# First queries and keys of three branches made as block products, their placing behind the last merge, and a first projection tile that begins with the high parts

## What is computed

```python
def token_mixer(x, w_in, b_forget, sinks, w_branch, w_gate, b_gate, w_out):
    (aq, ak, av, bq, bk, bv, cq, ck, cv, ciq, cik, ciw, dq, dk, dv, df) = jnp.split(x @ w_in, offsets, axis=-1)
    o_a = banded_attention(...)      # sliding window, 8 query heads, 2 key heads
    o_b = dilated_attention(...)     # three dilations, 8 heads
    o_c = dsa_attention(...)         # top 256 keys by an indexer, one key head for 8 queries
    o_d = forgetting_attention(...)  # causal, with a cumulative log forget gate
    proj = jnp.einsum('bsnk,nkd->bsnd', branches, w_branch)
    gates = jax.nn.sigmoid(x @ w_gate + b_gate).reshape(b, L, N_BRANCH, D_MODEL)
    merged = jnp.sum(gates * proj, axis=2)
    return merged @ w_out

def reference(x, ...):
    x = layer_norm(DEEPNORM_ALPHA * x + token_mixer(x, ...), ln1_g, ln1_b)
    return layer_norm(DEEPNORM_ALPHA * x + conv_glu_ffn(x, ...), ln2_g, ln2_b)
```

## Time and profile before

| | |
|---|---|
| median of 3 runs | 2093.48 us (2091.12 to 2094.64) |
| profiled execution | 2093.97 us, its span 2092.2 us |
| mean granted clock of PE | 0.999 |
| PE busy | 2060.4 us, 98% |
| DVE, ACT, POOL busy | 1536.4, 968.5, 937.3 us |
| share of PE in the chain that ended last | 87% |

### The profile page before, as it was taken

The page is one execution under the profiler, slowest core; times in us unless marked ns, Lnnn a source line. Parts: engine busy times, 40 slices in busy tenths (PEclk is TensorE's granted clock), DMA queues, the critical chain, the costliest instruction groups (busy, mean ns, idle before and its releaser), DMA issues.

```text
span 2092.2 us, 28999 instructions
## 1 busy us (share of the span) xinstructions
PE 2060.4 (98%) x10382; PEld 1727.0 (83%) x10382; DVE 1536.4 (73%) x2549; ACT 968.5 (46%) x1740; POOL 937.3 (45%) x796
## 2 busy tenths in 40 slices
PE   9999999999999999999999999999999999999998
PEld 7788888888888888888888888888788888888887
DVE  8678887777686666797785666668877777775668
ACT  5543334566615556615635666523433333344540
POOL 4287752333322223324523333524756565645651
PEclk9999999999999999999999999999999999999999
DMA  4233323110042111230031000441566665558862
GB/s 132 72 111 110 101 91 62 31 31 21 26 152 64 50 32 51 75 100 28 22 121 31 21 21 11 141 161 61 180 181 203 191 192 161 171 189 310 270 215 92
DMA packets 197373, 224.26 MB, mean 107 GB/s; under 512 B 25704, under 2 KB 149608, under 8 KB 197232
## 3 DMA queue, kind: packets, MB, share of 16 engines
q1 hardware_dynamic: 194320, 212.43, 32.7%
q10 hardware_dynamic: 2912, 10.00, 1.3%
HBM read 164.17 MB, written 58.23 MB: 106 GB/s over the span
## 4 chain that ended last, share of the span: by engine, by line
PE 87%; DVE 7%; issue 2%; ACT 2%; POOL 1%; DMA 0%; DVEq 0%; ACTq 0%; POOLq 0%
PE pair L1359 13%; PE pair L927 13%; PE pair L911 7%; PE pair L1225 7%; PE obank L1359 5%; PE pair L1388 5%; PE obank L1021 4%; PE chunk L1000 4%; PE pair L1318 3%; PE chunk L1388 3%; PE obank L1225 3%; PE pair L972 3%; PE pair L973 3%; PE pair L1271 2%; PE obank L1388 2%
## 5 line engine op out<-in xcount | busy, mean ns | idle before, releaser
L2175 POOL TENSOR_TENSOR w_lo<-w_raw,w_hi 128x1024 fp32r<-128x1024 f32 x64 | 159.5, 2492 | 311.1 <-ACT w_hi L1652 311.0
L1675 ACT ACTIVATE pt_hi<-chunk 128x512 fp32r<-128x512 f32 (+1 forms) x272 | 150.8, 555 | 179.2 <-PE chunk L1000 177.8
L2578 DVE TENSOR_TENSOR pt_lo<-chunk,pt_hi 128x512 fp32r<-128x512 f32 (+1 forms) x272 | 173.2, 638 | 80.1 <-ACT pt_hi L1675 75.7
L2230 POOL TENSOR_SCALAR prob<-prob,att 128x256 f32<-128x256 f32 (+4 forms) x172 | 118.1, 696 | 198.5 <-DVE att L2514 198.2
L927 PE MATMUL pair<-act_hi,w_hi 128*128 128x512 f32 x432 | 186.4, 432 | 2.5 <-DVE heads L2519 2.3
L927 PE MATMUL pair<-act_hi,w_lo 128*128 128x512 f32 x432 | 170.0, 393 | 0.0
L927 PE MATMUL pair<-act_lo,w_hi 128*128 128x512 f32 x432 | 169.4, 392 | 0.0
L2399 DVE TENSOR_SCALAR_CACHE_REDUCE o_top<-score,stat 128x384 uint8<-128x384 f32 (+1 forms) x186 | 167.0, 941 | 0.5
L1021 PE MATMUL obank<-pt_hi,heads 128*128 128x256 f32 (+1 forms) x568 | 148.4, 285 | 0.6 <-DVE pt_lo L2578 0.6
L1777 ACT ACTIVATE prob<-prob,att 128x257 f32<-128x257 f32 (+6 forms) x172 | 120.5, 702 | 39.3 <-DVE att L2504 38.0
L1021 PE MATMUL obank<-pt_lo,heads 128*128 128x256 f32 (+1 forms) x568 | 138.6, 281 | 0.0
(11 more groups left out here) (489 smaller groups left out, 5932.5 us busy)
## 6 DMA issues: line engine op xcount, KB each, us to landing
down_sums<-dn_sums SPq DMA_DIRECT2D x40, 512.0 KB, 6.4
w_raw<-in_w_in SPq DMA_DIRECT2D x37, 512.0 KB, 3.8
gates<-o_t SPq DMA_DIRECT2D x22, 512.0 KB, 2.9
up_raw<-in_w_up SPq DMA_DIRECT2D x22, 512.0 KB, 4.8
gate_raw<-in_w_ffn_gate SPq DMA_DIRECT2D x22, 512.0 KB, 6.0
hidden<-gelu_s SPq DMA_DIRECT2D x22, 512.0 KB, 3.3
dn_raw<-down_sums SPq DMA_DIRECT2D x44, 256.0 KB, 4.1
h_in<-down_sums SPq DMA_DIRECT2D x44, 256.0 KB, 4.8
```

The costliest lines, as they stand in the source:

```text
L2175: nc.gpsimd.tensor_tensor(split_into(1, g), w_raw[:, g % 2, 0:kt * cols], split_into(0, g).bitcast(F32), ALU.subtract).then_inc(lo_ready, 1)
L2578: nc.vector.tensor_tensor(pt_lo[:, n % PT_SLOTS, 0:m], t[:, 0:m], pt_hi[:, n % PT_SLOTS, 0:m].bitcast(F32), ALU.subtract).then_inc(chunk_f ...
```

## The change

Six more tiles join `GATE_TILES`: for D, A and C the first pair's queries and the first pair's keys (for C the keys and values), so that `NGATE` is 14. ACT copies them without the sigmoid, SP stores them in a tensor `first_heads` and loads the two of a branch back into `o_t[:, 0]` and `o_t[:, 1]` during the merge before. The steps `q`, `k` and `kv_c` of D, A and C become one step `heads`, in which PE does nothing: behind the last matmul of a merge it goes straight to the value tile (D, A) or to the transposes (C). ACT and DVE place high and low parts from `o_t` in pieces, and PE waits for the semaphore `first_placed` ahead of the scores of units 0, 4 and 8.

Around this, the last gated tile of B's, D's and A's merge is done by DVE behind the first placed pieces; gate tiles 6 and 7 go to other places of `o_t` and are loaded later; ACT's `ahead()` in the value step of D and A stands between the exponentials of units 0 and 1, and in C ahead of them; A's first bias lies elsewhere; the whole top-k search is done in the gates stage and the distances in the merges. C's filler table loses four parts, and nine instead of four go ahead of its first units. In `project_parts` the mode `low_last` sorts each half by product: all high by high, then high by low, then low by high, each with a wait of its own.

The core of the diff:

```diff
-TOPK_GATES = {1: 2, 6: 2, 2: 2, 5: 2, 7: 2, 3: 2, 4: 2}
-TOPK_MERGE = {B: (2, 3), D: (1, 2), A: (0, 1), C: (0, 0)}
-TOPK_FIRST = {("k", D): 7, ("q", D): 6, ("k", A): 5, ("q", A): 5}
-SEARCH_PARTS = 191
-DISTANCE_PARTS = 6
+TOPK_GATES = {1: 3, 6: 2, 2: 2, 5: 2, 7: 2, 3: 2, 4: 2}
+SEARCH_PARTS = 191 + NSC
+DISTANCE_PARTS = 5
+MERGE_ROWS = {B: 3, D: 2, A: 1}
+MERGE_PARTS = {B: (8, 2), D: (4, 1), A: (3, 1)}
...
-BESIDE_C = (((0, 0), (0, 2), (1, 1), (1, 1), (2, 2), (3, 0), (3, 1), (6, 0), (6, 2), (8, 1),
+BESIDE_C = (((0, 0), (3, 0), (3, 1), (6, 0), (6, 2), (8, 1),
...
-FIRST_C = 4
+FIRST_C = (4, 5)
...
-GATE_TILES = [(br, dt) for br in BRANCH_ORDER for dt in STORED_GATES[br] if (br, dt) not in FILLER_GATES]
+HEAD_TILES = [(what, br) for br in BRANCH_ORDER[1:] for what in ("q", "k")]
...
-        if br == C:
-            out += [("kv_c",)]
-        if br == A:
-            out += [("k", A, 0)]
-        out += [("q", br, 0)]
-        if br in (B, D):
-            out += [("k", br, 0)]
+        out += [("q", br, 0), ("k", br, 0)] if br == B else [("heads", br)]
         out += [("v_c",)] if br == C else [("v", br, 0)]
...
-                        order.sort(key=lambda kn: kn[1] == 2)
+                        order.sort(key=lambda kn: kn[1])
...
-                        if low_last and s == 0 and (k, n) == (0, 2):
+                        if low_last and (k, n) == (0, 0):
+                            pe.wait_ge(act_part, NTOK if s == 0 else 2 * NTOK)
+                        elif low_last and (k, n) == (0, 1):
+                            pe.wait_ge(*((x_taken, NTOK) if s == 0 else (x_low, NTOK)))
...
-                    fill(FIRST_C)
+                    fill(FIRST_C[0])
+                    pe.wait_ge(first_placed, placed_first(br, 1))
                     scores(br, pr, 0)
                     scores(br, pr, 1)
+                    fill(FIRST_C[1])
...
+                        if p == 0 and br != B and u in (4, 8):
+                            pe.wait_ge(first_placed, placed_first(br, u // 4 + 1))
...
+            def load_heads(br):
+
+                at = BRANCH_ORDER.index(br) - 1
+                if at == 0:
+                    sp.wait_ge(merge_free, 4)
+                else:
+                    sp.wait_ge(sum_done, sums_of(BRANCH_ORDER[at]) + 4)
+                for what in ("q", "k"):
+                    tile = GATE_TILES.index((what, br))
+                    sp.wait_ge(gate_stored[tile % 2], 16 * (tile // 2 + 1))
+                    sp.dma_start(first_head(what), tile_kept((what, br))).then_inc(heads_loaded, 16)
 
             def load_gate_tile(br, dt):
...
+            def gate_made_of(n, k, dst, src):
+
+                tile = GATE_TILES[2 * n + k]
+                if tile in HEAD_TILES:
+                    return nc.scalar.activation(dst, src, ACT.Copy)
+                return nc.scalar.activation(dst, src, ACT.Sigmoid, bias=gate_bias_of(*tile))
...
+            def first_heads(br):
+
+                at = BRANCH_ORDER.index(br)
+                act.wait_ge(merge_full, NKT * at)
+                act.wait_ge(heads_loaded, 32 * at)
+                first_half(br, 0)
+
+            def first_half(br, s):
+
+                q_hi(br, 0, 0, first_head("q")[0:HD, half_cols(s)], half_cols(s))
+                k_hi(0, first_head("k")[0:HD, half_cols(s)], cols=half_cols(s))
+
+            def other_heads(br):
+
+                first_half(br, 1)
+                q_hi(br, 0, 1, first_head("q")[HD:P, :])
+                if br != C:
+                    k_hi(1, first_head("k")[HD:P, :])
+                if br == D:
+                    act.wait_ge(merge_free, merge_at(B) + NKT)
+                    spill(NKT - 1)
+                if br == C:
+                    ahead()
+
...
                     tiles[1].next()
-                    for u in range(2):
-                        exps(step[1], step[2], u)
+                    exps(step[1], step[2], 0)
+                    if step[1] != B:
+                        ahead()
+                    exps(step[1], step[2], 1)
...
+                    gated(A, NKT - 1)
                     inverse(br, 0)
+                    first_half(br, 1)
                 if pr == 0:
                     biased(br, pr, 2)
                     biased(br, pr, 3)
+                if (br, pr) == (C, 0):
+                    other_query(br).then_inc(first_placed, 1)
                 if beside_v(br, pr):
...
+            def first_half(br, s):
+
+                q_lo(br, 0, 0, first_head("q")[0:HD, half_cols(s)], half_cols(s))
+                k_lo(0, first_head("k")[0:HD, half_cols(s)], cols=half_cols(s)).then_inc(first_placed, 1)
+
...
+                elif kind == "heads":
+                    first_half(step[1], 0)
+                    if step[1] != C:
+                        first_half(step[1], 1)
+                        gated(BRANCH_ORDER[BRANCH_ORDER.index(step[1]) - 1], NKT - 1)
...
+                    biased(step[1], step[2], 0)
+                    if step[1] != B:
+                        other_query(step[1])
+                        k_lo(1, first_head("k")[HD:P, :], (0,))
+                    biased(step[1], step[2], 1)
+                    if step[1] != B:
+                        k_lo(1, first_head("k")[HD:P, :], (1,)).then_inc(first_placed, 1)
+                    inverse(step[1], 0)
```

More of the change, by code:

```diff
@@ L794, in gate_bias_of, with tile_weights, tile_kept, first_head @@
             return gate_bias[:, br * NKT + dt:br * NKT + dt + 1]
+        def tile_weights(tile):
+            if tile not in HEAD_TILES:
+                return w_tile(w_gate[0], tile[0] * D_MODEL + tile[1] * P, P)
+            what, br = tile
+            return w_tile(w_in[0], Q_COL[br] if what == "q" else CK if br == C else K_COL[br], P)
+        def tile_kept(tile):
+            return heads_dram[HEAD_TILES.index(tile)] if tile in HEAD_TILES else gates_dram[tile]
+        def first_head(what):
+            return o_t[:, 0 if what == "q" else 1, :]
+        def placed_first(br, part):
+            return 3 * (BRANCH_ORDER.index(br) - 1) + part
         gate_out = [o_t[:, 2, :], o_t[:, 3, :]]
@@ L1073, in attention @@
                         pe.wait_ge(chunk_free, chunk_base[1])
+                        if pr == 0 and merge_tiles.n:
+                            pe.wait_ge(merge_free, merge_tiles.n)
                     if g >= 2:
@@ L1518, in _ @@
                                  allow_slow_non_contiguous=True).then_inc(late_params, 16)
+                if step[0] == "heads":
+                    for source in ring_sources(("v", step[1], 0)) if step[1] != C else ():
+                        load_weights(source)
+                    load_heads(step[1])
+                    if step[1] == D:
+                        forget_bias(0)
+                        forget_bias(1)
+                    for dt in range(GATE_HOMES, NKT):
+                        load_gate_tile(BRANCH_ORDER[BRANCH_ORDER.index(step[1]) - 1], dt)
                 for n, source in enumerate(ring_sources(step)):
-                    if step in (("q", B, 0), ("k", B, 0)):
+                    if step in (("q", B, 0), ("k", B, 0), ("v", D, 0), ("v", A, 0)):
                         continue
@@ L1524, in _ @@
                     if step[0] == "merge":
-                        for dt in {3: range(1, 4), 4: (4,)}.get(n, ()) if step[1] == FINAL else {3: range(1, 6), 4: (6, 7)}.get(n, ()):
+                        for dt in {3: range(1, 4), 4: (4,)}.get(n, ()) if step[1] == FINAL else {3: range(1, 6)}.get(n, ()):
                             load_gate_tile(step[1], dt)
@@ L2299, in _ @@
                                                     ).then_inc(sum_done, 1)
-                    split_weights(min(needed + 2, len(ring_list)) - ring.n)
+                    if br == D:
+                        pool.wait_ge(sum_done, sums_of(D) + 2)
+                        for j in range(PROB_SLOTS):
+                            set_sinks(0, j)
+                        pool.wait_ge(sum_done, sums_of(D) + NKT - 1)
+                        make_bias(0)
+                    split_weights(min(needed + (2 if br == FINAL else 1), len(ring_list)) - ring.n)
+                elif step[0] == "heads":
+                    pass
                 elif step[0] == "attn":
@@ L2421, in topk_search @@
                 own(nc.vector.tensor_tensor(cand, low, marks[0], ALU.bitwise_xor))
+                yield
+                for i in range(FIRST_TOPK, NTOK):
+                    b = i - FIRST_TOPK
+                    own(nc.vector.tensor_scalar(junk[:, 0, 0:(i + 1) * P], score[:, SC_OFF[i]:SC_OFF[i] + (i + 1) * P],
+                                                cand.bitcast(F32)[:, b:b + 1], None, ALU.is_gt, ALU.add,
+                                                accum_out=count[:, b:b + 1]))
+                    if b < NSC - 1:
+                        yield
             marks = [chunk[0][:, 8 * k:8 * k + NSC].bitcast(U32) for k in range(2)]
@@ L2969, in merged_lo @@
                     def merged_lo(k):
```

(16 more changed lines are left out.)

207 lines of the change are left out of this document (86 added, 121 removed).

## The result

| | before | changed |
|---|---|---|
| median | 2093.48 us (7 runs, 2091.12 to 2094.64) | 2100.13 us (7 runs, 2097.92 to 2101.56) |
| ratio of the times | 1 | 1.0035, 95% interval 1.0025 to 1.0045 |
| span and mean clock of the profiled execution | 2092.2 us, 0.999 | 2097.8 us, 0.995 |

The forecast was 2092.2 in a range of 2086.5 to 2097.5. The kernel became 6.6 us slower, beyond the range, and the interval of the ratio does not reach 1.

The account below looks back on a forecast made before the run. TensorE, busy 98% of the span, was taken as the bound. Terms -8.2 - 1.0 + 1.7 + 2.2 + 4.0 = -1.3 us took 2093.5 to 2092.2, no measurable change, in a range of 2086.5 to 2097.5.

Parts of the forecast that it names:

- Saved matmuls: Six tiles leave the entries and return as three gates-stage pairs: 36 matmuls fewer on PE, -8.2 us.
- Gates stage with more search: Three more pairs and more top-k search on DVE; PE still sets the pace at 19.04 us a pair, 0.
- Start: First projection tile: PE waits for ACT's high parts alone and the second half's wait goes, -1.0 us.
- Entry of D: DVE's last key tile, blocked by POOL's split, delays the normalisation; PE waits 2.1 us, +1.7 net.
- Entry of A: D's chain with one more DVE sum, the addition of D's last tile; PE waits 2.7 us, +2.2 net.
- rival 1: Saving arrives nearly whole: POOL's split misses DVE's key tile, C's filler covers more; 2086.5 to 2087.4 us, chance 0.28.
- Entry of C: ACT places heads before exponentials, DVE's reciprocal waits; PE waits 3.1 us before unit 4, +4.0 us in all.
- the clock's term: Lower PE clock behind the new waits at D, A and C; left out of the forecast's sum.
- rival 2: New waits at D, A and C bring clock falls of 1.7 us each, a second in C; 2099.0 us, chance 0.14.
- one part more done: At C's entry, one more projection part is finished before unit 7, credited with 0.7 us.

Follow-up runs that it names:

- e4: The kernel before with only the new order of the first projection tile; 2091.97 us, ratio to before 0.9996 (0.9987 to 1.0005).
- e2: The changed kernel with ScalarE's next weight split at D and A moved behind the first six copies; 2097.14 us, ratio to before 1.0024.
- e7: e6 with DVE's last key tile at D and A, and A's addition, behind the reciprocal, and C's addition later; 2092.64 us, ratio to before 1.0001.
- e1: The changed kernel with extra, overwritten matmuls keeping TensorE busy in the waits at the entries of D, A and C; 2096.76 us, ratio to before 1.0021.
- e3: The changed kernel with C's second half placed ahead of the reciprocal and the next weight's split later; 2097.78 us, ratio to before 1.0023.
- e5: The changed kernel with one filler part less in C's first pair, 23 instead of 24; 2096.99 us, ratio to before 1.0024.
- e8: e6 with the additions of D's and A's last tiles moved into the attention behind; 2088.15 us, ratio to before 0.9975 (0.9965 to 0.9985).
- e6: The changed kernel with the edits of e2, e3 and e5 together; 2089.96 us, ratio to before 0.9988 (0.9979 to 0.9997).

## Why the prediction was wrong

- *Saved matmuls, -8.2:* right. PE has 36 matmuls fewer, and the first transposes of B come 55.72 us later than before, which is three pairs (57.12) less the start's gain.
- *Gates stage with more search, 0:* right; PE has no gap in 266.5 us.
- *Start, -1.0:* 1.4 in the trace. The size was a little low. The median of e4 shows 0.9.
- *Entry of D, +1.7:* the mechanism is right, and so is the length, 1.92 us for 2.1 foretold, in part by luck: POOL's split was put from 9.6 to 12.5 us though 9.6 + 2.4 is 12.0; it began later, at 10.0, and ended at 12.4. e2 shows the collision. The Trainium skill ("SBUF — State Buffer", section "Who interferes with whom") states that of a DVE instruction with two SBUF inputs and a GpSimd one that reads SBUF, the first to start holds the other up; the rows of D agree (2.70 us for 1.22), and e7's agree in the other direction (1.85 and 2.81 us for 0.83).
- *Entry of A, +2.2:* right in kind, a wait of 3.33 instead of 2.7. The addition took the 1.23 us foretold. What the term left out, though rival 1 names it, is that DVE can hold POOL up as well: the split, begun behind a DVE tile, took 3.15 us instead of 2.40, and the key tile ended only after it.
- *Entry of C, +4.0:* right in place and kind (3.1 foretold, 3.53 measured). Without a fall of the clock unit 7 came 20.57 us behind the merge (e1): with the one part more taken off, +4.9 against +4.1.
- *The step that failed most:* the forecast took the clock's term at 0 and priced it as rival 2, with 0.14. In the changed kernel's profile the clock fell behind all three new waits. e1 puts that at 1.5 + 1.5 + 0.8 us, near the rival's 1.7 each at D and A, less in C, where DVE's waits hide it. The wait of 1.73 us at the start, which left the clock alone, weighed too much: it was one case.
- *The step that failed second:* "one part more done" was counted as 0.7 us won at C's entry, and the stream of parts was not followed to its end. There it costs 2.5 us of wait and, in the traces of e1, e2 and e3, a fall of the clock. e5 shows it: 3.1 us in the median, 1.8 in the trace.

Together: the forecast's -1.3, the clock's 3.8 and the late wait's 2.5 make +5.0 of the +6.6; by this sum neither of the two alone would have left the range. Longer waits at A and C (0.6 and 0.8) and small losses in B's merge and A's attention are of the size of the rest. The two traces, 5.6 us apart in span, give another sum: net of the 21.8 us of matmuls that each entry lost, the stages of D, A and C are 2.6, 5.1 and 8.3 us longer, where 1.7, 2.2 and 4.0 were foretold, and the part behind C, which is unchanged, is 1.1 shorter in this execution. Rival 1 was right in one thing: the saving is there to be had. e8 gets 4.9 us of the 9.6 (8.2 and the start's 1.4) with the waits shortened but not gone. The 0.2% under which the forecast saw no measurable change was too wide: for e6's 0.12% the interval still leaves out 1.

## What to carry to other kernels

When work leaves the engine that sets the pace, the chain that it had covered comes to light: price that chain on every engine, and count with a lower clock behind each wait that is as long as one which already shows such a fall (here 1.7 us), though not every execution pays it. When a list of filler parts is edited, count its sum, since one part more or less shifts every later part against the buffers that it waits for. Two engines that hold each other up can't be sorted by moving one instruction a little; put one of them beside work that does not take part.

## What the runs showed of the hardware that was not expected

The same wait brings a fall of PE's clock in one execution and none in another. The wait of 3.04 us near the end of C left the clock at 1.00 in the changed kernel's profile and was followed by six microseconds at 0.50 in e3's. The wait of 1.88 us at A was followed by a fall in e2 and by none in e6 (the first two lines: e2, e6). And a wait of 1.7 us in A's attention, which all ten profiles have, was followed by a fall in eight, as in the earlier trace rows, and by none in e1's and e8's (the last two lines: e8).

```profile
969.00:973.00 4.00, 3.70 (x14) 0.57 0.00 0
966.00:974.00 8.00, 5.83 (x33) 1.00 0.00 0
...
1041.06 0.50 PE L929 MATMUL pair<-act_hi,w_hi 128*128 128x512 f32 x1 [1.71 <-DVE heads L2590]
1040.00:1048.00 8.00, 6.94 (x41) 1.00 0.00 0
```

The Trainium skill ("TensorE: Matmul & The Clock Gate", "Part 1: The HAM clock gate") states that the gate looks at how busy PE has been; the length of the wait alone does not decide here. The spread of some 4 us among the runs of one kernel goes with it: of the kernel before's 31 runs beside e1 to e4, the 11 with a mean clock of 0.999 have a median of 2091.47 us, the 11 with 0.997 one of 2093.65. What decides in which execution a fall comes was not tried.
